# Expert weights in pieces of 1 MB, and products that go piece by piece over both column banks

## What is computed

```python
def ec_moe(h, w_router, w_gate, w_up, w_down):      # 16 experts, 1024 x 1024 matrices
    cap = EC_CAPACITY_FACTOR * n // N_EXPERTS        # 64 tokens per expert
    aff = softmax(h @ w_router)
    g, idx = top_k(aff.swapaxes(1, 2), cap)          # each expert chooses its tokens
    xs = h[idx]
    a = silu(einsum('becd,edf->becf', xs, w_gate)) * einsum('becd,edf->becf', xs, w_up)
    y = einsum('becf,efd->becd', a, w_down) * g[..., None]
    return zeros.at[idx].add(y)
```

## Time and profile before

| | us |
|---|---|
| three runs | 2303.33, 2306.80, 2307.02 |
| median | 2306.8 |
| profiled execution, its own time | 2305.65 |
| span of that execution, first to last instruction | 2303.8 |
| mean granted TensorE clock | 0.983 of 2.4 GHz |
| TensorE busy | 2214.8 (96%) |
| VectorE / ScalarE busy | 985.7 / 393.1 |
| bytes read from HBM | 561.36 MB |

### The profile page before, as it was taken

How to read it: one execution, slowest core, us unless ns; L and a number is a source line. 1 busy time by engine, 2 the same in 40 slices (tenths; PEclk the granted TensorE clock), 3 DMA queues, 4 the chain that set the end, 5 groups by cost and what they waited for, 6 DMA issues and landing times.

```text
span 2303.8 us, 24836 instructions
## 1 busy us (share of the span) xinstructions
PE 2214.8 (96%) x10134; PEld 1288.5 (56%) x10134; DVE 985.7 (43%) x1358; ACT 393.1 (17%) x748; POOL 68.3 (3%) x84
## 2 busy tenths in 40 slices
PE   7999999999999999999899999999999899999998
PEld 3343588888884456764544444445885544444443
DVE  3883397788835641861322212215541311112223
ACT  3224312012123111751100000002000200000000
POOL 1100100000020000001000000001001000000000
PEclk9999999999999999999899999999999899999999
DMA  9316244777531112031599999998211399999996
GB/s 352 137 41 256 73 146 150 252 270 275 184 137 38 37 37 85 5 132 72 208 425 428 429 428 428 428 428 312 73 73 73 129 419 428 428 428 428 428 428 272
DMA packets 108186, 564.55 MB, mean 245 GB/s; under 512 B 8776, under 2 KB 17614, under 8 KB 80974
## 3 DMA queue, kind: packets, MB, share of 16 engines
q1 hardware_dynamic: 107680, 563.35, 61.1%
q10 hardware_dynamic: 430, 0.13, 0.0%
HBM read 561.36 MB, written 2.10 MB: 245 GB/s over the span
## 4 chain that ended last, share of the span: by engine, by line
PE 80%; DMA 13%; DVE 4%; ACT 1%; issue 1%; SPq 1%; DVEq 0%; ACTq 0%
PE psum L1872 21%; PE psum L1469 20%; PE psum L1223 14%; DMA ring<-in_moe_w_gate_dram 9%; PE psum L1919 5%; PE psum L1962 5%; PE psum L1664 3%; PE psum L1785 2%; DMA ring<-in_mlp_w_dram 2%; PE psum L1416 2%; PE psum L1716 1%; DMA ring<-in_conv_w_pw_dram 1%; PE psum L1743 1%; PE psum L1733 1%; DMA ring<-in_ada_w_dram 1%
## 5 line engine op out<-in xcount | busy, mean ns | idle before, releaser
L1872 PE MATMUL psum<-ring,arena 128*64 128x512 f32 x3072 | 669.3, 593 | 19.9 <-DMA ring<-in_moe_w_gate_dram 18.2
L1872 PEld LDWEIGHTS psum<-ring,arena 128*64 128x64 f32 x3072 | 224.5, 137 | 450.2 <-issue 447.9
L1223 PE MATMUL psum<-hT,ring 128*128 128x512 f32 x608 | 266.3, 596 | 3.8 <-DMA ring<-in_conv_w_pw_dram 3.8
L1223 PEld LDWEIGHTS psum<-hT,ring 128*128 128x128 f32 x608 | 115.7, 191 | 149.1 <-issue 140.8
L2628 DVE SCALAR_TENSOR_TENSOR xT<-psum,modv,xT 128x512 f32<-128x512 f32 x128 | 96.1, 751 | 231.3 <-PE psum L1962 219.3
L1469 PE MATMUL psum<-ring 128*128 128x256 f32 x640 | 142.9, 380 | 3.6 <-DVE rstd L2314 3.4
L1469 PE MATMUL psum<-hT,ring 128*128 128x256 f32 x608 | 140.2, 388 | 0.8 <-ACT hT L812 0.8
L1469 PEld LDWEIGHTS psum<-ring 128*128 128x128 f32 x640 | 121.0, 190 | 23.4 <-issue 7.2
L1919 PEld LDWEIGHTS psum<-arena 128*128 128x128 f32 x1024 | 121.4, 198 | 14.0 <-issue 14.0
L1469 PEld LDWEIGHTS psum<-hT,ring 128*128 128x128 f32 x608 | 118.1, 195 | 18.9 <-issue 2.2
L1919 PE MATMUL psum<-arena 128*128 128x128 f32 x1024 | 125.6, 283 | 2.5 <-DVE arena L2636 2.5
(11 more groups left out here) (345 smaller groups left out, 2306.8 us busy)
## 6 DMA issues: line engine op xcount, KB each, us to landing
ring<-in_moe_w_gate_dram SPq DMA_DIRECT2D x64, 2048.0 KB, 14.4
ring<-in_moe_w_up_dram SPq DMA_DIRECT2D x60, 2048.0 KB, 15.8
ring<-in_moe_w_down_dram SPq DMA_DIRECT2D x60, 2048.0 KB, 17.2
ring<-in_ada_w_dram SPq DMA_DIRECT2D x24, 2048.0 KB, 8.6
ring<-in_mlp_w_dram SPq DMA_DIRECT2D x16, 2048.0 KB, 8.7
ring<-in_w_mod_dram SPq DMA_DIRECT2D x12, 2048.0 KB, 12.6
ring<-in_conv_w_in_dram SPq DMA_DIRECT2D x6, 2048.0 KB, 19.2
ring<-in_attn_w_in_dram SPq DMA_DIRECT2D x5, 2048.0 KB, 7.9
```

What stands on the lines that cost most here:

```text
L1223: ins = pe.matmul(bank[:, 0:width], w[:, k, col:col + P], src(k), start=start and k == 0, stop=stop and k == kts - 1)
L1872: ins = pe.matmul(psum[64 * e:64 * e + 64, bank + nh, :], src[:, 4 * h + k, 64 * e:64 * e + 64], w[:, k, nh * N:(nh + 1) * N], start=h == ...
```

## The change

The quarter pieces and `DOWN_PIECES` go away. Every block, in every pair, is loaded as two pieces of 1 MB: rows k = 0, 1 (8 KB in each partition, on semaphore `landed`) and rows k = 2, 3 (on a second semaphore per slot, `landed_late`). SyncE issues the first piece of both experts and then the second piece of both. TensorE multiplies the first piece into both banks, then the second piece into both banks, waiting for each piece on its own, and signals after each piece (`gate_freed`, `up_freed`, `down_freed`, three per product, and `_done` per bank for the last). SyncE waits for these signals piece by piece. The loop of loads runs over all pairs but the first, and the loop of products is as before without the special cases.

```diff
-DOWN_PIECES = [(0, 2, "down_first"), (2, 3, "down_second"), (3, 4, None)]
...
-                def load_half(i, m, w, half, name, value):
-
-                    sp.wait_ge(S[name], value)
+                def load_piece(i, m, w, half, piece):
+
                     for e in range(2):
                         slot = (s0 + 2 * m + e) % RING
-                        src = w[bass.ds(2 * i + e, 1), :, half, :]
-                        sp.dma_start(ring[:, slot * BLK:(slot + 1) * BLK], src.rearrange("e p n -> p (e n)"))\
-                            .then_inc(landed[slot], 16)
...
-                given_back(2)
-                load_half(0, 2, up, 0, "down_done", 2 * first + 1)
-                for k in range(4):
-                    sp.wait_ge(S["gate_quarter"], 4 * layer + k + 1)
-                    load_piece(0, 3, up, 1, k, k + 1, "up_pieces" if k < 3 else None)
...
-                    load_half(i, 0, gate, 0, "up_done", 2 * n + 1)
-                    load_half(i, 1, gate, 1, "down_half", n + 1)
-                    load_half(i, 2, up, 0, "down_done", 2 * n + 1)
-                    load_half(i, 3, up, 1, "gate_half", n - layer)
-                    load_half(i, 4, down, 0, "gate_done", 2 * n + 2)
-                    load_half(i, 5, down, 1, "up_half", n + 1)
...
+                        src = w[bass.ds(2 * i + e, 1), :, half, 2 * D * piece:2 * D * (piece + 1)]
+                        at = slot * BLK + 2 * D * piece
+                        sp.dma_start(ring[:, at:at + 2 * D], src.rearrange("e p n -> p (e n)"))\
+                            .then_inc((landed_late if piece else landed)[slot], 16)
+
+                def load_pair(i, n, first=False):
+
+                    if first:
+                        for m, (w, half) in enumerate(((gate, 0), (gate, 1), (up, 0))):
+                            given_back(m)
+                            for piece in range(2):
+                                load_piece(i, m, w, half, piece)
+                    else:
+                        sp.wait_ge(S["up_freed"], 3 * n)
+                        load_piece(i, 0, gate, 0, 0)
+                        sp.wait_ge(S["up_done"], 2 * n + 1)
+                        load_piece(i, 0, gate, 0, 1)
+                        sp.wait_ge(S["down_freed"], 3 * n - 2)
+                        load_piece(i, 1, gate, 1, 0)
+                        sp.wait_ge(S["down_freed"], 3 * n - 1)
+                        load_piece(i, 1, gate, 1, 1)
...
+                    sp.wait_ge(S["gate_freed"], 3 * n + 1)
+                    load_piece(i, 3, up, 1, 0)
+                    sp.wait_ge(S["gate_freed"], 3 * n + 2)
+                    load_piece(i, 3, up, 1, 1)
...
+                load_pair(0, PAIRS * layer, True)
+                with sp.Fori(1, PAIRS) as i:
+                    load_pair(i, i + PAIRS * layer)
...
-                        for nh in range(2):
-                            ins = product_step(ws, bank, src, h, nh, range(4))
-                            if h == 1:
-                                ins.then_inc(S[name + "_done"], 1)
-                        if h == 0:
-                            ins.then_inc(S[name + "_half"], 1)
+                        for piece in range(2):
+                            ws = weights(i, m, h, piece)
+                            for nh in range(2):
+                                for k in range(2 * piece, 2 * piece + 2):
+                                    for e, w in enumerate(ws):
+                                        ins = pe.matmul(psum[64 * e:64 * e + 64, bank + nh, :],
+                                                        src[:, 4 * h + k, 64 * e:64 * e + 64],
+                                                        w[:, k, nh * N:(nh + 1) * N], start=h == 0 and k == 0,
+                                                        stop=h == 1 and k == 3, skip_group_check=True)
+                                if h and piece:
+                                    ins.then_inc(S[name + "_done"], 1)
+                            if not (h and piece):
+                                ins.then_inc(S[name + "_freed"], 1)
```

More of the change, by code:

```diff
@@ L409, in block_kernel @@
         landed = [sem(f"landed{i}") for i in range(RING)]
+        landed_late = [sem(f"landed_late{i}") for i in range(RING)]
         for name in (
@@ L424, in block_kernel @@
             "hot_ready", "gsel_ready", "gathered", "xs_act", "xs_dve", "gselT_done", "gselT_sb",
[L425 removed]
+            "gate_freed", "up_freed", "down_freed", "gate_done", "up_done", "down_done", "sil_ready", "a_ready", "aT_done", "aT_act", "aT_dve",
             "y_act", "y_dve", "scattered", "acc_added",
@@ L533, in load_piece @@
[L533 to L541, removed]
@@ L1383, in mod_turn @@
                 ins.then_inc(S["mod_turned"], 1)
-            for name in ("up_done", "down_half", "down_done", "gselT_done"):
+            for name in ("up_done", "down_done", "gselT_done"):
                 pe.sem_inc(S[name], 1)
@@ L1857, in experts, with weights @@
                     pe.wait_ge(FREE[e], [v for x, v in tile_free[:t + 1] if x == e][-1])
-                def weights(i, m, h):
+                def weights(i, m, h, piece):
                     ws = []
@@ L1863, in weights, with products @@
                         slot = (s0 + 2 * (m + h) + e) % RING
-                        ws.append((landed[slot], 32 * i + 16 * (MOE_LOADS[layer][slot] + (2 * (m + h) + e) // RING + 1),
-                                   carve(ring, slot * BLK, 4, D)))
-                    return ws
[L1868 to L1877, removed]
+                        nth = (2 * (m + h) + e) // RING + 1
+                        if piece:
+                            pe.wait_ge(landed_late[slot], 32 * i + 16 * (2 * PAIRS * layer + nth))
+                        else:
+                            pe.wait_ge(landed[slot], 32 * i + 16 * (MOE_LOADS[layer][slot] + nth))
+                        ws.append(carve(ring, slot * BLK, 4, D))
+                    return ws
+                def products(i, bank, m, src, name, second=None):
                     for h in range(2):
@@ L1880, in products @@
                             pe.wait_ge(*second)
[L1881 to L1896, removed]
-                                for nh in range(2):
-                                    ins = product_step(ws, bank, src, h, nh, range(k0, k1))
-                                    if not done:
-                                        ins.then_inc(S[name + "_done"], 1)
-                            continue
@@ L1923, in gather, with gate @@
                     ins.then_inc(S["gathered"], 1)
-                def gate(i, n, pieces=None):
+                def gate(i, n):
                     pe.wait_ge(S["xs_act"], n + 1)
-                    products(i, 0, 0, xsT, "gate", (S["xs_dve"], n + 1), pieces=pieces)
+                    products(i, 0, 0, xsT, "gate", (S["xs_dve"], n + 1))
                 def turn_half(n, half):
@@ L1943, in turn_gsel, with down @@
                     ins.then_inc(S["gselT_done"], 1)
-                def down(i, n, pieces=None):
+                def down(i, n):
                     pe.wait_ge(S["aT_act"], n + 1)
@@ L1950, in down @@
                     pe.wait_ge(S["y_dve"], n + 1)
-                    products(i, 4, 4, aeT, "down", pieces=pieces)
+                    products(i, 4, 4, aeT, "down")
                 def scatter(n):
@@ L1968, in experts @@
                 pe.wait_ge(S["a_ready"], 2 * first + 1)
-                gate(0, first, "freed")
+                gate(0, first)
                 with pe.Fori(0, PAIRS - 1) as i:
                     n = i + first
-                    products(i, 2, 2, xsT, "up", pieces="added")
+                    products(i, 2, 2, xsT, "up")
                     gather(n + 1, 0)
@@ L1987, in experts @@
                 turn_half(last, 1)
-                down(PAIRS - 1, last, "landed")
+                down(PAIRS - 1, last)
                 scatter(last)
```

26 lines of the change are left out of this document (12 added, 14 removed).

## The result

The changed kernel takes 2313.72 us in the median of 10 runs (2309.96 to 2317.01), the kernel before 2306.64 in 10 runs (2303.33 to 2308.82): a ratio of 1.0032, 95% interval 1.0024 to 1.004. It is 7.1 us slower. Forecast were 2315.7 us and a range of 2307 to 2325. The profiled execution took 2312.31 us (span 2310.5), 6.7 us more than the one of before.

What follows compares the result with a forecast made beforehand. Transfers were taken to bound the expert loops, DMA share 1.01 at 428 GB/s. Layer 0 was to lose 4.6 us and layer 1 4.3, so 2306.8 + 8.9 = 2315.7 us, range 2307 to 2325.

Steps and rivals of the forecast that it cites:

- TensorE's work at no cost: Both expert loops: no matmul is added and the added semaphore waits lie under matmuls already issued; cost 0.
- SyncE's queue at no cost: Expert loops: 24 issues per pair in place of 12 take 12 us of 58.7; cost 0.
- The speed of the stream: Expert loops: 8 KB rows make a 2 MB block take 4.98 us against 4.893, with bounds of 4.93 and 5.05.
- rival B: Expert loops: 8 KB rows cost nothing, a block stays at 4.893 us, so faster, 2300 us; chance 0.06.
- The start of the stream: First pair of a layer: first load issued 1.73 us later, at 1123.85; the stream starts at 1128.2.
- slow ramp: First loads into a layer's empty queue: reaching full rate loses between nothing and 2.4 us; 0.5 taken.
- The end: End of layer 0: last piece lands at 1576.4, then 0.14 + 3.47 us; down ends at 1580.0, 4.6 us later.
- The sum of a layer: Expert loop from gate to down's end: 459.85 us, 4.6 us more in layer 0 and 4.3 in layer 1.
- Rival A: Expert loops: slot hand-back sets the pace, so handing back sooner saves 7.6 us per layer, 2292 us; chance 0.05.
- D: Expert loops: each DMA costs its own time in a full queue, 0.1 us each, 18 per layer, 2352; chance 0.06.
- C: Expert loops: blocks of 4.93 to 4.955 us shift layers 0 to 2.3 us each, 2307 to 2311; chance 0.17.
- forecast proper: Expert loops: blocks between 4.96 and 5.05 us, start cost and ramp within bounds, 2311.4 to 2328 us; chance 0.66.

Runs made afterwards that it cites:

- run with the order alone: Kernel before, loads unchanged, each half's products going over both banks for k = 0, 1, then for k = 2, 3: 2306.92 us, ratio 1.0007.
- run with quarters: Changed kernel with the first pair's hand-back row by row and up's second half loaded as 512 KB quarters, as before the change: 2315.45 us, ratio 1.0038.
- run with joint transfers: Changed kernel with one 2 MB transfer for both experts' pieces in 8 KB rows, 12 per pair and not 24: 2313.31 us, ratio 1.0033.
- fastest kernel: Changed kernel with pieces only for first loads, gate's second half, down's last block, and last pair's up second and down first half; rest whole: 2300.13 us, ratio 0.9975.

## Why the prediction was right

The sign, the mechanism and the size held: 8.9 us forecast, 7.1 measured, with the slower stream as the cause. Two terms were helped by chance, as the points on the speed and on the start say. By its steps:

- *TensorE's work at no cost.* Right, shown by the run with the order alone (1.0007) and by 27.69 us for 128 records.
- *SyncE's queue at no cost.* Right: with 12 or 24 issues per pair the time is the same (2313.31 and 2313.72).
- *The speed of the stream.* Predicted 4.98 us a block, from two windows of 4 to 5 us in the kernel before that gave 4.98 and 4.96; measured 59.64 / 12 = 4.970, or 2.097 / 0.422 = 4.969. The term is 90 x 0.076 = 6.9 us per layer, where 7.8 was forecast. This 0.9 us is most of the difference. So short a window can be further off: in the kernel before, 1154 to 1160 us gives 434 GB/s where the stream runs at 428. That both windows came within 1 GB/s of the 422 was luck, as the rival B had warned; at 428 the sum would have turned round.
- *The start of the stream.* Predicted 8.05 us after the first product (1128.2 - 1120.15). From the last landing, 1575.3 - 90 x 4.970 - 1120.57 = 7.4 (7.6 with 4.968 us a block). The first issue was placed right, 3.7 us after the first product; from there to the stream it took 3.7 to 3.9 us, so the 0.5 taken for a slow ramp was not there. The step put the first issue 1.73 us later than before and did not say what that does to the stream. Counted in the same way, the stream of the kernel before begins 1570.1 - 90 x 4.893 - 1120.15 = 9.6 us after the first product, so the changed one begins some 2 us sooner although it is issued later. The sum used only the absolute place of the stream and so was not hurt. That the stream would come sooner than before stood in these numbers (1128.2 against 1129.7) but not in the argument. The run with quarters points the same way: the changed start is the better one by 1.5 to 2.0 us per layer.
- *The end.* Predicted 3.61 us from the last landing to the scatter, measured 1579.02 - 1575.3 = 3.7. The run with smaller last pieces gives 1.0 and 1.7 us of it back. Beside that, the last landing itself now sets the end of the layer, where before it came 3.6 us early: from the first product it moved from 449.95 to 454.73 us, 4.8 later, which is about the 6.9 of the blocks less the 2 of the start.
- *The sum of a layer.* 459.85 us forecast, 458.45 measured: 0.9 less for the blocks, 0.6 less for the start, 0.1 more for the end.

What was predicted for the page also came: 422 GB/s (420 to 423 was said) at a share of 1.01, 59.64 us a round (59.8), and 59.64 - 57.45 = 2.2 us of idle time per round (2.3), of which the trace lists 1.98 as two waits. TensorE's bare round is shorter than the 57.45 of the prediction: 57.22 us in the two rounds without a wait (1156.84, 1214.06, 1271.28). Rival A (the hand-back sets the pace) fell with the first window: slots are freed 3.5 us sooner and the round got longer. B (rows of 8 KB cost nothing) fell with the 422 GB/s, and D (each transfer costs time of its own) with the run with joint transfers, which kept that rate with half the transfers. C (blocks of 4.93 to 4.955 us, 2307 to 2311) missed the block by 0.015 us and the time by 2 us. The range of the forecast proper, 2311.4 to 2328, is narrower than the bounds that it names: blocks of 5.05 us alone give 2315.7 + 2 x 90 x 0.07 = 2328.3, before any of the start. The Trainium skill's 2.0 us per transfer (DMA: Bandwidth & Descriptors, Anatomy of one DMA, a fit for transfers that GpSimd issues) plays no part in this full queue of SyncE's: 1 and 2 MB transfers gave 422 GB/s in 8 KB rows, 2 and 4 MB transfers 428 in 16 KB rows.

## What to carry to other kernels

Where the DMA share is 1.0, splitting a transfer along its rows slows every round, by a fixed price per row, and can pay only where something waits for part of a block and the stream does not set the pace anyway. Here that was the blocks of the last pair. At the first load into an empty queue pieces of 1 MB did better than pieces of 512 KB; whole blocks were not run there. A cut in every round at the block that TensorE waits for gave nothing by itself (58.88 us a round and not 58.72); whether the fastest kernel needs its cut at gate in the middle rounds was not run. After each cut look for the next whole block that TensorE meets, because the wait moves on to it. Compare the stretch from the first product to the last as well as the medians: it is free of where the layer begins, but one execution's length still differed by up to 1 us between kernels with the same stream.

## What the hardware showed that was not expected

- The price of a row is the same from 16 to 8 KB and from 8 to 4 KB, 0.57 to 0.60 ns each in the stream (an estimate of 9 to 10 ns on one of 16 engines), while the number of transfers does not show at all: 24 or 12 per pair in 8 KB rows (422 GB/s), 12 or 6 in 16 KB rows (428).
- A queue filled by 512 KB transfers from empty took longer to reach its rate than by 1 MB transfers: the same 4 MB are complete 17.9 us after the layer's first product with a first issue at 2.0, and 16.1 us after it with a first issue at 3.7.
